# A two-layer diffusion step on one core: layer 1's expert choice reordered on all engines, context tokens chosen in the latent tokens' last rounds, and the experts' last context rows added densely

## The reference, cut to what matters

```
def expert_choice_ffn(x, w_router, w_gate, w_up, w_down):
    t = x.reshape(b * n, d)
    cap = CAPACITY_FACTOR * (b * n) // N_EXPERTS
    aff = jax.nn.softmax(jnp.einsum('td,de->te', t, w_router), axis=-1)
    g, idx = lax.top_k(aff.T, cap)
    xe = t[idx]
    hid = silu(einsum('ecd,edf->ecf', xe, w_gate)) * einsum('ecd,edf->ecf', xe, w_up)
    ye = jnp.einsum('ecf,efd->ecd', hid, w_down) * g[..., None]
    out = jnp.zeros_like(t).at[idx.reshape(-1)].add(ye.reshape(-1, d))
...
        x = x + g1 * mix
        h = rmsnorm(x, p['norm2']) * (1 + sc2) + sh2
        x = x + g2 * expert_choice_ffn(h, ...)
```

## Time and profile before

| What | Value |
|---|---|
| time, median of 3 runs | 2243.1 us (2241.53 to 2243.93) |
| the profiled execution's own time | 2244.18 us |
| its span in the trace | 2241.6 us |
| mean granted PE clock | 0.952 of full speed |
| PE busy | 2039.0 us, 91% of the span |
| PEld busy | 1429.5 us, 64% |
| DVE busy | 858.7 us, 38% |
| ACT busy | 468.8 us, 21% |
| POOL busy | 165.4 us, 7% |

### The profile page before, as it was taken

How to read it: one execution, slowest core, us unless ns; L and a number is a source line. 1 busy time by engine, 2 the same in 40 slices (tenths; PEclk the granted TensorE clock), 3 DMA queues, 4 the chain that set the end, 5 groups by cost and what they waited for, 6 DMA issues and landing times. The chain is left out here.

```text
span 2241.6 us, 27543 instructions
## 1 busy us (share of the span) xinstructions
PE 2039.0 (91%) x11435; PEld 1429.5 (64%) x11435; DVE 858.7 (38%) x1802; ACT 468.8 (21%) x922; POOL 165.4 (7%) x155
## 2 busy tenths in 40 slices
PE   5999999979999999997899999993995399999996
PEld 2777767755666664442787777871442287878784
DVE  2244455356566662346222222214445622222221
ACT  1222221235656661122000000002132100000000
POOL 0000000000000000001101111111010101111111
PEclk9999999989999999997899999996997599999998
DMA  9201101167444315733858787837021866878771
GB/s 353 83 33 38 54 30 39 32 138 278 174 163 170 117 66 167 267 129 132 309 191 314 251 307 263 298 98 244 30 113 57 342 224 230 299 262 303 264 262 28
DMA packets 158060, 400.86 MB, mean 179 GB/s; under 512 B 12561, under 2 KB 30408, under 8 KB 151794
## 3 DMA queue, kind: packets, MB, share of 16 engines
q1 hardware_dynamic: 140962, 339.84, 42.1%
q0 software_dynamic: 16976, 59.29, 9.3%
HBM read 337.10 MB, written 62.00 MB: 178 GB/s over the span
## 5 line engine op out<-in xcount | busy, mean ns | idle before, releaser
L1884 PE MATMUL experts_gu<-experts_h_t,weights_w_gate 128*128 128x160 f32 x2048 | 302.8, 301 | 4.2 <-issue 4.2
L1884 PEld LDWEIGHTS experts_gu<-experts_h_t,weights_w_gate 128*128 128x128 f32 x2048 | 288.8, 192 | 19.2 <-issue 19.2
L1884 PE MATMUL experts_gu<-experts_h_t,weights_w_up 128*128 128x160 f32 x2048 | 299.9, 300 | 0.0
L1884 PEld LDWEIGHTS experts_gu<-experts_h_t,weights_w_up 128*128 128x128 f32 x2048 | 286.2, 191 | 0.0
L1908 PE MATMUL experts_dn<-weights_w_down,experts_hid 128*128 128x512 f32 x512 | 225.8, 594 | 0.0
L1949 DVE TENSOR_TENSOR experts_hid<-experts_act,experts_gu 128x160 f32<-128x160 f32 x128 | 41.1, 321 | 480.1 <-ACT experts_act L1938 480.1
L513 PE MATMUL proj_cv<-proj_h_t,proj_w_in 128*128 128x256 f32 x960 | 213.9, 381 | 2.6 <-DVE proj_h_t L710 2.6
L1938 ACT ACTIVATE experts_act<-experts_gu 128x160 f32<-128x160 f32 x128 | 39.0, 304 | 830.6 <-PE experts_gu L1884 830.6
L513 PEld LDWEIGHTS proj_cv<-proj_h_t,proj_w_in 128*128 128x128 f32 x960 | 182.6, 192 | 29.3 <-issue 4.7
L1908 PEld LDWEIGHTS experts_dn<-weights_w_down,experts_hid 128*128 128x128 f32 x512 | 94.7, 190 | 113.9 <-issue 113.9
L997 PE MATMUL attn_sc<-attn_keys_s,attn_q_s 96*128 96x512 f32 (+1 forms) x384 | 155.6, 541 | 3.8 <-DVE attn_pr_t L1130 2.8
(11 more groups left out here) (395 smaller groups left out, 2122.7 us busy)
## 6 DMA issues: line engine op xcount, KB each, us to landing
weights_w_gate<-w_gate_l SPq DMA_DIRECT2D x32, 2048.0 KB, 9.5
weights_w_up<-w_up_l SPq DMA_DIRECT2D x32, 2048.0 KB, 16.9
weights_w_down<-w_down_l SPq DMA_DIRECT2D x32, 2048.0 KB, 21.5
attn_w_mod<-w_mod_l SPq DMA_DIRECT2D x40, 1024.0 KB, 6.4
proj_w_in<-w_in_l SPq DMA_DIRECT2D x3, 2048.0 KB, 19.6
proj_x<-x POOLq DMA_DIRECT2D x10, 512.0 KB, 3.8
weights_w_down<-x SPq DMA_DIRECT2D x10, 512.0 KB, 4.7
layer_room_a<-w_mod_l SPq DMA_DIRECT2D x4, 1024.0 KB, 10.2
```

The source lines that it names most:

```text
L1884: last = pe.matmul(gu[j % 2][:, m * SLOTS:(m + 1) * SLOTS], w[u][:, k, j * P:(j + 1) * P], h_t[u][:, k, :], start=(k == 0), stop=(k == KD ...
```

## The change

It has three parts.

1. **`Choice`, both layers.** The context tokens' affinities go to rows 64 to 79 of the tile `left`, which has 80 rows now. Rounds 0 to 13 take the latent rows as before, rounds 14 and 15 take all 80 rows at once, and rounds 16 and 17 take only the 16 context rows, over 256 columns. So there are 18 rounds in place of 16 and 4.
2. **`fourier_and_choice`, layer 1.** The context products' copies move from ACT to DVE (9 copies in 4 groups instead of 5, each group in its own bank). On PE pair 3's turn, routing and turning of logits stand right behind the context products; `middle(0)` is cut in two around the turn of the affinities, and pair 4's even and odd products come behind both. ACT copies the first 16x512 of the affinities beside DVE's copies (`keep_near`), loads its Sqrt table early and copies both halves of pair 4's turned tiles. On DVE `middle(0)` moves from before the rounds to behind round 2, pair 4's two outputs behind rounds 3 and 5, its root behind round 7.
3. **`experts`, both layers.** The last four `scatter_prompt` are gone. Instead SP loads a table of token numbers (one row of 256 numbers to all partitions) when expert 14's last gate and up product is done. DVE compares it with the chosen places and so makes a 128x256 matrix of ones and zeros (`find_places`, between expert 15's first two `hidden`). SP loads the 256 context rows (1 MB) when the scatters of experts 0 to 11 have landed. PE multiplies the matrix with the 128 weighted rows (`add_up_rows`: four products of 128x512, after expert 15's down product). DVE adds the sums to the loaded rows (four adds of 128x512), and SP stores them (two stores of 512 KB).

```
     def rounds(...):
-            src = left if r else self.aff[c]
+            rows = slice(0 if r < self.ROUNDS else self.FIRST_P, self.ROWS if r < self.JOINT else self.ALL)
+            cols = slice(0, DEC // 2 if r < self.ROUNDS else SEQ)
+            src = self.left[rows, cols] if r else self.aff[:]
...
# experts: SP
+                sp.wait_ge(gu_full, KF * (NE - 1))
+                sp.dma_start(token, t["token"].partition_broadcast(P)).then_inc(token_in, 16)
+                sp.wait_ge(yp_out, 16 * (NE - BATCH))
+                sp.dma_start(prompt_rows, t["x1"][0].rearrange("(n p) d -> p n d", p=P)).then_inc(rows_in, 16)
+                for n in range(PT):
+                    sp.wait_ge(rows_ready, 2 * (n + 1))
+                    sp.dma_start(t["x1"][0][n * P:(n + 1) * P, :], prompt_rows[:, n, :]).then_inc(rows_out, 16)
...
# experts: PE, at the end
+                def add_up_rows():
+                    pe.wait_ge(places_ready, 1)
+                    pe.wait_ge(yp_ready, 2 * NB)
+                    pe.wait_ge(tp_kept, sample_turns(NE - 1, 1) + 1)
+                    for n in range(PT):
+                        for half in range(2):
+                            pe.matmul(sums[2 * n + half][:], places[:, n * P:(n + 1) * P], yp[:, half * BANK:(half + 1) * BANK],
+                                      start=True, stop=True).then_inc(sums_full, 1)
...
# experts: DVE
+                def find_places():
+                    dve.wait_ge(token_in, 16)
+                    dve.tensor_copy(place, per.at_p4[:, NB - 1:NB]).then_inc(place_ready, 1)
+                    dve.wait_ge(place_ready, 1)
+                    dve.tensor_scalar(places, token, place, None, ALU.is_equal).then_inc(places_ready, 1)
...
+                            dve.tensor_tensor(prompt_rows[:, n, cols], prompt_rows[:, n, cols], sums[2 * n + half][:], ALU.add).then_inc(rows_ready, 1)
...
# fourier_and_choice: DVE
-                middle(0)
                 choice.divide(dve, ch, 1)
                 choice.keep_affinities(dve, ch, 1)
-                choice.rounds(dve, ch, 1, 0, 1)
+                choice.rounds(dve, ch, 0, 3)
+                middle(0)
+                choice.rounds(dve, ch, 3, 4)
                 output(last + 1, 0)
-                choice.rounds(dve, ch, 1, 1, 4)
+                choice.rounds(dve, ch, 4, 6)
                 output(last + 1, 1)
-                choice.rounds(dve, ch, 1, 4, 6)
+                choice.rounds(dve, ch, 6, 8)
                 root(last + 1)
-                choice.rounds(dve, ch, 1, 6, 8)
-                turned(last + 1)
...
```

More of the change, by code:

```diff
@@ L1274, in prepare_tables @@
     def prepare_tables(self, dve):
-        for tile in (self.bias, self.pads[0], self.pads[1], self.aff[1]):
+        for tile in (self.bias, self.pads[0], self.pads[1], self.aff):
             dve.memset(tile[:], 0.0)
+        dve.memset(self.left[:], -1.0)
         dve.wait_ge(self.w_r_in, 16)
@@ L2006, in _ @@
                         rows_sample(e, half)
+                dve.wait_ge(rows_in, 16)
+                for n in range(PT):
+                    for half in range(2):
+                        rows_added(n, half)
 def fourier_and_choice(nc, t, per, weights):
@@ L2195, in product, with middle @@
                     last.then_inc(full, 1)
[L2197 removed]
+                def middle(c, lo, hi):
                     use, k = middle_use(c), KP + HS if c else HP
                     wait(pe, eo_kept, use - 1)
[L2201 removed]
+                    for g in range(lo, hi):
                         for half in range(2):
@@ L2289, in _ @@
                 for m, results in enumerate(context_products()):
-                    wait(pe, kept, N_FIRST + m - 3)
-                    product(bank(m % 4), results)
+                    product(bank(m), results)
                 i = PAIRS - 2
                 turn(i, 0)
-                pe.wait_ge(kept, N_FIRST + N_CONTEXT)
-                middle(0)
                 turn(i, 1)
                 router(i, 0)
-                even(i + 1, 0)
                 router(i, 1)
                 choice.turn_batch(pe, 0)
-                odd(i + 1, 0, 0, GROUPS)
                 choice.turn_batch(pe, 1)
-                even(i + 1, 1)
+                pe.wait_ge(kept, N_FIRST + N_CONTEXT)
+                middle(0, 0, 2)
                 choice.turn_affinities(pe, 1)
-                odd(i + 1, 1, 0, GROUPS)
+                middle(0, 2, GROUPS + 1)
+                for half in range(2):
+                    even(i + 1, half)
+                    odd(i + 1, half, 0, GROUPS)
                 turn(i + 1, 0)
@@ L2504, in _, with move @@
                     output(i, 1)
-                    root(i)
+                    if i < PAIRS - 2:
+                        root(i)
                 last = PAIRS - 2
+                context = list(context_products())
+                def move(lo, hi):
+                    for m in range(lo, hi):
+                        dve.wait_ge(full, N_FIRST + m + 1)
+                        for n, (dst, cols, _) in enumerate(context[m]):
+                            done = dve.tensor_copy(dst, bank(m)[0:dst.shape[0], cols])
+                            if n < len(context[m]) - 1:
+                                ch.add(done)
+                        ch.settle()
+                        done.then_inc(kept, 1)
+                move(0, 2)
+                root(last)
+                move(2, N_CONTEXT)
                 turned(last)
@@ L2606, in _tables @@
     partner[0, 0:2] = SEQ // 2, DEC // 2
+    tables["token"] = np.arange(SEQ, dtype=np.float32)
     tables["partner"] = partner.astype(np.uint32)
```

141 lines of the change are left out of this document (79 added, 62 removed).

## The result

The changed kernel takes 2214.56 us (median of four runs, 2208.95 to 2217.45) against 2243.51 (2241.53 to 2245.04): a ratio of 0.9869, 95% interval 0.9842 to 0.9897, so 29 us less (23 to 35). The profiled execution took 2208.95 with a span of 2207.2, 5.6 under the median. It was a lucky one, as the experiments show; its stretches count, not its total.

A forecast was written before the change was run, and what follows sets the result against it. PE bounds the experts except at their ends, DVE layer 1's choice, with SP's weight loads ending that stage after the change. 2244.18 − 18.0 (choice) − 7.0 (tails) = 2219.2, forecast 2219 us, range 2212 to 2229.

The forecast's parts named there:

- Up to the first round: Layer 1's choice, pair 3's first normalised rows to first round (stretch A): 30.5 us before, first round 19.2 earlier.
- The added 2.6: Ahead of layer 1's first round: pair 3's slow second turn and exposed copies cost 2.6 us, bounds 1.0 and 4.3.
- removed 21.8: Layer 1's choice before the first round: late turn, PE's and DVE's products and copy share removed, together 21.8 us.
- From the first round to the end: Layer 1's choice: DVE needs 54.3 us after the first round, but SP's weight loads end the stage at 1753.4.
- The tails: End of the experts, both layers: dense last rows save 3.5 us per layer (2.4 to 4.9), 7.0 for both.
- the compromise for the second store: End of the experts: stores end at 2230.3 alone or 2232.9 with the second queued behind; 2231.8 taken between.
- Layer 0's choice: Layer 0: shorter rounds give nothing, since DVE's last tables wait 6.97 us for PE.
- SP held the end: Layer 1's choice; the rival was that SP doesn't hold the end: gain 21.1 us, time 2216, chance 0.13.
- the tails gave more, not less: End of the experts; the rival was that the dense tail gives nothing: time 2226, chance 0.08.
- the table landed: Expert 15; the rival was a late token table, over 0.2% slower from a landing of 34.7 us on: chance 0.04.
- nothing queued behind the weights: Start of layer 1's experts; the rival was gathers queued behind weights by 3.9 us: time 2223, chance 0.04.
- the rival of the low clock: Layer 1's choice, PE at 1.2 GHz: part of the products 2223 to 2227, chance 0.16; all 2237, chance 0.03.

The follow-up runs named there:

- products ahead: Changed kernel with the rest of PE's middle row and pair 4's first even and odd products again ahead of the affinities' turn; first round 21.5 us after pair 3's normalised rows.
- the three kernels above: Changed kernel with expert 1's weights issued later, context rounds apart, or both: first gather 55.5, 60.2 and 57.5 us after the first round, against 59.0 to 59.9.
- the changed kernel's second run: The changed kernel rerun unchanged for a second trace and more times: 2213.95 us, ratio 0.9869 to the kernel before beside it.

## Why the prediction was right, step by step

The time lies in the range (2212 to 2229), 4.4 below the point. The order of events is the forecast one.

- **Up to the first round**: A is 10.4 to 10.7 in six traces and 11.3 in two, 11.3 forecast (9.7 to 13.0). The added 2.6 counted with the slow clock in pair 3's second turn. In the two traces at 11.3 the clock was 0.50 in both turns, in the other six it was higher in part (1.09 and 1.50 us for eight turns each in the first). So the point was met where the clock stayed low, and where it did not the 2.6 was 0.7 too much. Of the removed 21.8, the products of 512 columns put back by "products ahead" are confirmed as one sum. The late turn's 2.6, DVE's `middle`, the second `even` and ACT's share of the copy were not tried one by one; the fall of A from 30 to 10.5 shows them only together with the rest.
- **From the first round to the end**: DVE's last table comes 53.7 after it (54.3 forecast). In the four traces of the whole choice with nothing else moved in it, SP's first issue comes at 35.6 to 36.0 (35.7), SP is held for 20.7 to 21.9 (21.7) and ends 2.9 to 4.2 behind DVE (3.1). That it holds the end is shown by the three kernels above. In all eleven traces with six loads SP's fifth and sixth issue end 0.2 to 1.8 and 0.5 to 2.0 us behind the landing of the second and the third load, which bears out that SP was held until data landed. Gain of the choice: 18.6 in place of 18.0.
- **The tails**: 4.3 and 4.5 in place of 3.5 each, within the 2.4 to 4.9. The mis-sized term is the compromise for the second store, which was put behind the scatter as what ends the stage; leaving it out changes nothing. The end went with the latent scatter, which took 6.7 to 7.1 to land and not the 6.0 of the prediction's earliest case. So the range held for another reason than the one given, and that 3.5 lies near is in part luck. The four products took 3.45 (3.6 forecast). That a store of this size takes 2.6 was wrong in this place (5.3 to 6.0). So would the estimate of 3.2 have been that the prediction worked out from the Trainium skill's page "DMA: Bandwidth & Descriptors", section "Anatomy of one DMA — SWDGE (gpsimd) path", whose figures are for GpSimd's path.
- **Layer 0's choice**: nothing by the edit, as forecast. The turn of its lists comes at 1051.8 to 1058.4 in the three traces of the choice before, and at 1050.7 to 1060.1 in the ten of the choice as changed.
- **The rivals**: SP held the end; pair 4's products ran at 2.4 GHz; the tails gave more, not less; the table landed after 4.1 to 4.8. The first gather of layer 1's experts landed within 7.6 us (1744.98, PE's first turn at 1752.55), against 7.8 before, and the time from it to the last down product is 441.4 and 442.5, before 442.7 and 442.2: nothing queued behind the weights. In the rival of the low clock the 6.4 us need all of the first output's products doubled (8.1, less a slack of 1.7), not up to half of them as it says.

18.6 + 8.8 = 27.4 by the stretches, against 25.0 forecast and 29 (23 to 35) measured: 2.4 of the 4.4 us by which the point was high are these two terms. Another 0.7 is that the sum started from an execution of 2244.18, and the kernel before has a median of 2243.51. The rest of 1.3 is less than what executions of one kernel differ by.

## What to carry to other kernels

Where a stage ends with a barrier, list for each engine when it would be done without the others: shortening the last one is worth only the distance to the next, and here that was an engine held in its DMA issues. The 2.0 us of the joint rounds were worth nothing until three loads had been moved over the barrier. And compare stretches between events of the same trace when totals scatter by more than the edit is worth.

## What the runs showed of the hardware

- The granted clock can be 0.50 for 10 us while PE is busy in all of them (the changed kernel's second run, 1580 to 1590), and 0.83 in the same 10 us of another execution. The Trainium skill's page "TensorE: Matmul & The Clock Gate", section "What's actually happening", has activity release the throttle; these rows show PE busy by the profile and the clock low all the same. In layer 1's mixer, the same 500 PE instructions were busy for 129.25 us at a mean clock of 0.92 and for 139.94 at 0.86. Over the thirteen traces the turn of layer 0's lists, counted from the start of the span, and the length of that stretch of the mixer differ by up to 9 and 11 us.
- A plain 512 KB store lands after 5.3 to 6.1 beside an accumulating scatter of 128 rows, and after 2.6 where the earlier trace rows were taken. The scatter lands after 6.7 to 7.2 beside the stores, and landed after 6.0 to 6.2 at the same place before.
- In the changed kernel a MAX8, FIND_INDEX8 or MATCH_REPLACE8 over 80 rows of 512 takes what one over 48 rows takes: 0.69, 0.68 and 0.67.
